# Feed-forward layers in two halves, with gate/up products of 512 columns over both parts of a normalised input

## The chip, the cores and the metric

The kernel runs on one NeuronCore of one Trainium2 chip. The time is the device time of one execution in microseconds (us), given as the median of several runs. The engines are TensorE (PE, with its weight loads shown apart as PEld), VectorE (DVE), ScalarE (ACT), GpSimd (POOL) and SyncE (SP, which issues most DMAs).

## What is computed

Two blocks of one model, 256 tokens (L) of width 1024 (D), in float32. Block one has four gated feed-forward layers around a Mamba-2 layer and a block-attention layer; block two has a conformer convolution, a sparse attention and, behind each, a feed-forward layer with a causal convolution of width 3. The part that matters here, cut from the reference:

```python
D_MODEL, SEQ, D_FF = 1024, 256, 2816

def modulate(x, g, c_act, w, b):
    m = c_act @ w + b                          # w: 1024 x 3072
    shift, scale, gate = jnp.split(m, 3, axis=-1)
    return rmsnorm(x, g) * (1.0 + scale[:, None, :]) + shift[:, None, :], gate[:, None, :]

def swiglu(h, w_gate, w_up, w_down):
    return (jax.nn.silu(h @ w_gate) * (h @ w_up)) @ w_down

# block one, for each of two depths: ffn, mixer (mamba2, then moba), ffn
h, g = modulate(x, norm_g[i, 0], c_act, mod_w[i, 0], mod_b[i, 0])
x = x + 0.5 * g * swiglu(h, ffn_w_gate[i, 0], ffn_w_up[i, 0], ffn_w_down[i, 0])

# block two, for each of two depths: mixer (conformer, then nsa), conv_ffn
def conv_ffn(h, w_up, w_dw, b_dw, w_down):
    a, v = jnp.split(h @ w_up, 2, axis=-1)
    return (jax.nn.silu(causal_dwconv(a, w_dw, b_dw)) * v) @ w_down
x = x + conv_ffn(rmsnorm_2(x, ffn_norm_g[i]), ffn_w_up[i], ffn_w_dw[i], ffn_b_dw[i], ffn_w_down[i])
```

## The kernel before

The residual X stays on the chip as eight tiles of 128 features by 256 tokens. Ten layers run one after the other: ffn0, ssm, ffn1, ffn2, moba, ffn3, conf, cffn0, nsa, cffn1; six of them are feed-forward layers (FFNs), the four gated ones of block one and the two with a convolution (cffn). All weights come as one stream of slots of 128x2048 float32 (1 MB), loaded by SP into a ring of six. An FFN takes 33 slots: 22 of gate/up (slot f holds the gate and the up columns of hidden tile f, of 22) and 11 of down.

**Precision by parts.** Each float32 operand is split into a high part of fewer bits and the rest. ACT writes w_hi of each slot (`high`, L1442), DVE writes w_lo (`low`, L1876), each into one of three buffers. A product is then three products that add up in PSUM: high by high, high weight by low input, low weight by high input. `woven` (L721) does this for gate and up together (six matmuls for each of eight k), `three` (L728, L729, L730) for down. All inputs have 256 columns, and in the gated FFNs 258: two further columns carry the shift of the modulation. "Triple" below means the three products of one weight tile.

**The input is not normalised ahead.** The gate/up products run on X times its gain (Hs_hi, Hs_lo); the sums of squares (L765) and the reciprocal root of each token (`rstd`, spread over the partitions by L709, written to `row` by ACT L1464) come while the first tiles are multiplied. ACT copies a finished tile from PSUM (L1456), POOL multiplies both halves by `row` (L651), ACT applies silu (L1473), DVE multiplies by the other half (L2086, or L2074 and following with the taps of the convolution), ACT rounds the result to hid_hi (L1477) and DVE writes hid_lo (L2095).

**Rounds.** After two gate/up slots and `clear` (L774: four matmuls of 512 bf16 columns that write zeros into the accumulators `acc`), a hardware loop runs rounds of two gate/up slots and one down slot; each down slot adds two hidden tiles into all eight output tiles in `acc`. All eight are finished in the last slot, and DVE then updates X.

**Folds.** The modulation vectors (c_act times a 1024x3072 matrix) are made on DVE beside this: a fold is two passes over 128x1024 (L1891) on a slot that POOL loads into a ring of its own (L568). In a round they stand after the slots 2, 4 and 7 of six (FOLD_AT).

The engines are ordered by hand, each by its own program text, and joined by semaphores: `split_ready` (weights split), `pair_free` (gate/up PSUM read), `hid_ready` (hidden parts written), `slot_done` (PE is done with a slot).

## Time and profile before

| quantity | value |
|---|---|
| median of 3 runs | 1868.75 us (1866.8 to 1869.99) |
| span of the profiled execution | 1865.1 us |
| PE busy | 1803.1 us, 97% of the span |
| DVE busy | 1323.5 us, 71% |
| ACT busy | 948.5 us, 51% |
| POOL busy | 377.5 us, 20% |
| DMA | 371.1 MB, mean 199 GB/s |

The profiled execution's span is 3.65 us under the median of the three runs. "Busy" of PE counts the time in which a matmul is in the array; records of neighbouring matmuls overlap, so the spacing of their starts says what one costs, and not the duration of a record. Idle time in brackets at a row's end is time in which the engine waited, with the instruction that released it.

### The profile page before, as it was taken

The page shows a single profiled execution, that of the slowest core. Times are in us where ns is not written, and L with a number is a line of the kernel's source. Part 1 is how long each engine was busy: PE and PEld are TensorE (multiplying, and loading weights), DVE is VectorE, ACT ScalarE, POOL GpSimd, SP SyncE. Part 2 cuts the span into 40 slices and gives each one's busy share as a digit, 9 for nine tenths or more (in the row PEclk, how much of TensorE's full clock was granted, in tenths as well). Part 3 has the DMA queues.
Part 4 walks back from the last instruction along what each step waited for, and adds up shares of the span by engine and source line. Part 5 has one row for each costly group of instructions (what it writes and reads, how often), then busy time and mean ns, then how long its engine had stood idle before and what let it go on. Part 6 is the DMA issues. An engine that isn't in the chain of part 4 may idle for free.

```text
span 1865.1 us, 36260 instructions
## 1 busy us (share of the span) xinstructions
PE 1803.1 (97%) x14574; PEld 1733.4 (93%) x14574; DVE 1323.5 (71%) x1824; ACT 948.5 (51%) x1357; POOL 377.5 (20%) x371
## 2 busy tenths in 40 slices
PE   3999999999999999999999999999999999999998
PEld 2999989979999999999889999988999989689998
DVE  6677877888767576768876555897666767866665
ACT  3554555474645465446465445316544533764453
POOL 1222200051222122211143221002222200431221
PEclk9999999999999999999999999999999999999999
DMA  9877835745577647675924554313555533134551
GB/s 376 319 274 279 324 113 181 277 151 226 184 290 264 256 179 293 253 279 177 372 92 161 188 191 180 142 62 114 177 183 180 180 143 133 41 109 167 191 187 67
DMA packets 51059, 371.10 MB, mean 199 GB/s; under 512 B 5664, under 2 KB 5664, under 8 KB 6048
## 3 DMA queue, kind: packets, MB, share of 16 engines
q1 hardware_dynamic: 41760, 302.85, 44.4%
q0 software_dynamic: 9216, 67.11, 9.2%
q8 instruction: 56, 0.92, 0.2%
q14 instruction: 27, 0.22, 0.0%
HBM read 368.89 MB, written 1.05 MB: 198 GB/s over the span
## 4 chain that ended last, share of the span: by engine, by line
PE 83%; DVE 10%; ACT 4%; issue 1%; DMA 1%; POOL 0%; POOLq 0%; SPq 0%; DVEq 0%; ACTq 0%
PE gu L721 39%; PE acc L729 8%; PE acc L728 8%; PE acc L730 8%; DVE arena L2424 3%; PE gu L1054 2%; PE gu L1193 2%; PE gu L728 2%; PE gu L730 2%; PE gu L729 2%; DVE w_lo L1876 2%; DMA mring<-in_mods 1%; DVE mring L1891 1%; DVE arena L2166 1%; PE acc L1264 1%
## 5 line engine op out<-in xcount | busy, mean ns | idle before, releaser
L1876 DVE TENSOR_TENSOR w_lo<-ring,w_hi 128x2048 fp32r<-128x2048 f32 x265 | 613.7, 2319 | 271.6 <-ACT w_hi L1442 271.5
L1442 ACT ACTIVATE w_hi<-ring 128x2048 fp32r<-128x2048 f32 x265 | 504.9, 1907 | 74.6 <-PE acc L730 49.3
L721 PE MATMUL gu<-Hs_hi,w_hi 128*128 128x258 f32 (+1 forms) x2112 | 427.8, 284 | 2.5 <-DVE Hs_lo L1940 1.3
L721 PE MATMUL gu<-Hs_lo,w_hi 128*128 128x258 f32 (+1 forms) x2112 | 423.1, 282 | 0.0
L721 PE MATMUL gu<-Hs_hi,w_lo 128*128 128x258 f32 (+1 forms) x2112 | 422.5, 281 | 0.0
L651 POOL TENSOR_TENSOR arena<-arena,rstd 128x512 f32<-128x512 f32 x132 | 201.0, 1523 | 831.1 <-ACT arena L1456 778.4
L721 PEld LDWEIGHTS gu<-Hs_hi,w_hi 128*128 128x128 f32 x2112 | 325.7, 189 | 4.8 <-issue 1.8
L721 PEld LDWEIGHTS gu<-Hs_hi,w_lo 128*128 128x128 f32 x2112 | 325.8, 189 | 0.0
L721 PEld LDWEIGHTS gu<-Hs_lo,w_hi 128*128 128x128 f32 x2112 | 325.4, 189 | 0.0
L729 PE MATMUL acc<-hid_lo,w_hi 128*128 128x256 f32 x1056 | 297.8, 282 | 0.0
L728 PE MATMUL acc<-hid_hi,w_hi 128*128 128x256 f32 x1056 | 296.4, 281 | 1.2 <-DVE hid_lo L2095 1.2
L730 PE MATMUL acc<-hid_hi,w_lo 128*128 128x256 f32 x1056 | 295.8, 280 | 0.0
L1477 ACT ACTIVATE hid_hi<-arena 128x256 fp32r<-128x256 f32 x132 | 55.2, 419 | 292.2 <-DVE arena L2086 201.6
L728 PEld LDWEIGHTS acc<-hid_hi,w_hi 128*128 128x128 f32 x1056 | 198.9, 188 | 1.5 <-issue 1.5
L730 PEld LDWEIGHTS acc<-hid_hi,w_lo 128*128 128x128 f32 x1056 | 199.4, 189 | 0.0
L729 PEld LDWEIGHTS acc<-hid_lo,w_hi 128*128 128x128 f32 x1056 | 198.4, 188 | 0.0
L1891 DVE SCALAR_TENSOR_TENSOR mring<-mring,cact 128x1024 f32<-128x1024 f32 x144 | 170.0, 1220 | 11.1 <-DMA mring<-in_mods 10.9
L1456 ACT ACTIVATE arena<-gu 128x516 f32<-128x516 f32 (+1 forms) x132 | 78.4, 594 | 138.2 <-PE gu L721 135.0
L728 PE MATMUL gu<-H_hi_ssm,w_hi 128*128 128x256 f32 x384 | 109.8, 286 | 4.9 <-DVE w_lo L1876 3.1
L2095 DVE TENSOR_TENSOR hid_lo<-arena,hid_hi 128x256 fp32r<-128x256 f32 x132 | 70.0, 530 | 57.6 <-ACT hid_hi L1477 57.6
L730 PE MATMUL gu<-H_hi_ssm,w_lo 128*128 128x256 f32 x384 | 108.4, 282 | 0.0
L729 PE MATMUL gu<-H_lo,w_hi 128*128 128x256 f32 x384 | 108.2, 282 | 0.0
(413 smaller groups left out, 2841.5 us busy)
## 6 DMA issues: line engine op xcount, KB each, us to landing
ring<-in_weights SPq DMA_DIRECT2D x276, 1024.0 KB, 4.8
mring<-in_mods POOLq DMA_DIRECT2D x64, 1024.0 KB, 6.1
mring<-in_mods SPq DMA_DIRECT2D x8, 1024.0 KB, 7.5
con<-in_constants SPq DMA_DIRECT2D x1, 1408.0 KB, 12.1
X<-in_x SPq DMA_DIRECT2D x1, 1024.0 KB, 7.2
out<-X SPq DMA_DIRECT2D x1, 1024.0 KB, 3.9
cact<-in_c SPq DMA_DIRECT2D x1, 512.0 KB, 3.3
vec<-in_vectors SPq DMA_DIRECT2D x1, 498.0 KB, 4.1
```

The lines of the kernel that those rows point to most:

```text
L651: pool.tensor_tensor(both, both, row.unsqueeze(1).to_broadcast([P, 2, L]), ALU.mult).then_inc(scaled_ready, 1)
L721: ins = mm(dst, part, x_lo if i == 1 else x_hi, start=start and i == 0, stop=stop and i == 2, skip_group_check=True)
L728: mm(dst, hi, x_hi, start=start, stop=False, skip_group_check=True)
L729: mm(dst, hi, x_lo, start=False, stop=False, skip_group_check=True)
L730: return mm(dst, lo, x_hi, start=False, stop=stop, skip_group_check=True)
L1442: act.activation(w_hi[buffer_of(n0, s)][:, :], ring[:, n % RING, :], ACT.Copy).then_inc(hi_ready, 1)
L1456: act.activation(c[:, :, 0:width], gu[:, 2 * (f % 2):2 * (f % 2) + 2, 0:width], ACT.Copy).then_inc(pair_free, 1)
L1477: act.activation(hid_hi[:, f % 4, :], a, ACT.Copy).then_inc(hid_hi_ready, 1)
L1876: dve.tensor_tensor(w_lo[b][:, :], ring[:, n % RING, :], w_hi[b][:, :].bitcast(F32), ALU.subtract).then_inc(split_ready, 1)
L1891: ins = dve.scalar_tensor_tensor(out=w, in0=w, scalar=1.0, in1=cact[:, :], op0=ALU.mult, op1=ALU.mult, accum_out=total)
L2095: dve.tensor_tensor(hid_lo[:, f % 4, :], o, hid_hi[:, f % 4, :].bitcast(F32), ALU.subtract).then_inc(hid_ready, 1)
L2424: ins = dve.scalar_tensor_tensor(out=part_sum, in0=UP[:, m, tap:tap + L], scalar=v1("w_dw", tap * KD + m), in1=part_sum, op0=ALU.mult, op1 ...
```

## The change

In all six FFNs the order of the slots, the form of the products and the place of the normalisation change.

- **Two halves.** Gate/up tiles 0 to 11, then six slots of down over them, gate/up 12 to 21, then five slots of down. Down runs output tile by output tile (`down_tiles`), each into one of four banks of `acc` (its columns 0 to 255), still by three products of 256 columns; `start=True` opens a bank, `clear` is gone. Each output tile is added to X twice (`partial`), once for each half. The hardware loops of the FFNs are unrolled.
- **512 columns.** Tiles 0 to 2 run as before, on the bare input, the third into two banks of `acc`. Meanwhile Hs_hi and Hs_lo are overwritten, k by k, by the parts of the normalised input (DVE `scaled` L2300, ACT `normal` L1646, DVE `normal_low` L2311). From tile 3 on (19 of 22), `paired` multiplies w_hi by both parts in one product of 512 columns (L837; an access pattern with a step from Hs_hi to Hs_lo) and w_lo by the high part in one of 256 (L839). The two halves of a PSUM bank are added later: ACT copies one to SBUF (`low_half` L1596), DVE adds the other (`add` L2284).
- **Other engines.** The multiplication of gate and up (L728 of the new kernel) and the low hidden part (L734) move from DVE to POOL; POOL's scaling by `row` (L718) remains for the three bare tiles. In the cffn layers the first tap moves from DVE to ACT.
- **Folds** stand at the slots of FOLD_SLOTS: in ffn0 16 of them, eight of these in the adjacent slots 19 to 26; in ffn1 and ffn2 12 each, with 19 to 22 and 24, 25 adjacent.
- **Ends of layers.** The squares and entries of the next layer and the splitting of its first two slots are placed in the last down slots. The diagonals of one of the three homes of the conformer's taps are built behind ffn3. Some buffers move, and the weight stream is packed in the new order.

```diff
-FOLD_AT = (2, 4, 7)
-LAST_FOLDS = (2, 3, 4, 5)
+FOLD_SLOTS = {"ffn0": (3, 5, 7, 9, 11, 13, 15, 17, 19, 20, 21, 22, 23, 24, 25, 26),
+              "ffn1": (5, 7, 9, 11, 14, 16, 19, 20, 21, 22, 24, 25),
+              "ffn2": (5, 7, 9, 11, 14, 16, 19, 20, 21, 22, 24, 25)}
+HALF_F0, HALF_N = (0, 12), (12, 10)
+DOWN_SLOT, DOWN_N = (12, 28), (6, 5)
...
+            def paired(bank, w, cols, x_both, x_hi, start, stop):
+                mm(bank.rearrange("p (a t) -> p a t", a=2), w_hi[w][:, cols], x_both, start=start, stop=False,
+                   skip_group_check=True)
+                return mm(bank[:, 0:L], w_lo[w][:, cols], x_hi, start=False, stop=stop, skip_group_check=True)
...
-                    pe.wait_ge(split_ready, s0 + s + 1 + it * 6)
-                    if f >= 2:
-                        pe.wait_ge(pair_free, f0 + f - 1 + it * 4)
+                    pe.wait_ge(split_ready, s0 + s + 1)
+                    pe.wait_ge(pair_free, f0 + (f - 2 if f < BARE_F + 2 else f - 1))
+                    for k in range(KD):
+                        if f == BARE_F:
+                            state["nh"] += 1
+                            pe.wait_ge(nh_ready, state["nh"])
+                        for e, cols in enumerate(columns(k)):
+                            ins = paired(bank[:, e, :], buffer_of(n0, s), cols, hs_twin(k), Hs_hi[:, k, 0:L],
+                                         start=(k == 0), stop=(k == KD - 1))
...
-                gate_up(1)
-                clear()
-                with pe.Fori(0, ROUNDS) as it:
-                    for s in (2, 5):
-                        gate_up(s, it)
-                        gate_up(s + 1, it)
-                        down(s + 2, (s - 2) // 3, it)
-                down(FSLOTS - 1, PAIRS - 1, last=True)
+                bare_gate_up(1)
+                bare_gate_up(2)
+                for f in range(BARE_F, HALF_F0[1]):
+                    gate_up(f)
+                down(0)
+                for f in range(HALF_F0[1], NF):
+                    gate_up(f)
+                down(1)
...
+                def low_half(f):
+                    act.wait_ge(slot_done, n0 + gu_slot(f) + 1)
+                    act.wait_ge(mul_ready, hid0 + f - 1)
+                    act.activation(cp[:, f % 2, :, 0:L], bank_of(f)[:, :, L:2 * L], ACT.Copy).then_inc(half_taken, 1)
...
+                def add(f):
+                    dve.wait_ge(half_taken, (NF - BARE_F) * i + f - BARE_F + 1)
+                    c = cp[:, f % 2, :, 0:L]
+                    dve.tensor_tensor(c, bank_of(f)[:, :, 0:L], c, ALU.add).then_inc(pair_free, 1)
...
+                for s in range(BARE_F, DOWN_SLOT[1]):        # DVE
+                    f = GU_TILE.get(s)
+                    if f is not None:
+                        add(f)
+                        low(n0, s + 2)
...
+                    fold_at(s)
```

PE at the start of ffn0 before, from the spread of the root on (names: w_hi_56 and w_lo_59 are one of the three pairs of buffers):

```order
L709 MATMUL acc<-con,rtok 128x128
L721 MATMUL gu<-Hs_hi,w_hi_55 128x258 x2
L721 MATMUL gu<-Hs_lo,w_hi_55 128x258 x2
L721 MATMUL gu<-Hs_hi,w_lo_58 128x258 x2
...
L774 MATMUL acc<-zeros 128x512 x3
L774 MATMUL acc<-zeros 128x512 [waits row_ready]
...
L721 MATMUL gu<-Hs_hi,w_hi_56 128x258 [waits pair_free]
L721 MATMUL gu<-Hs_hi,w_hi_56 128x258
L721 MATMUL gu<-Hs_lo,w_hi_56 128x258 x2
L721 MATMUL gu<-Hs_hi,w_lo_59 128x258 x2
```

And in the changed kernel, the end of the third tile and the start of the fourth (HL holds Hs_hi and Hs_lo):

```order
L824 MATMUL acc<-HL,w_hi_53 128x258 x4
L824 MATMUL acc<-HL,w_lo_56 128x258 x2
L837 MATMUL gu<-HL,w_hi_51 128x512 [waits nh_ready,pair_free,split_ready]
L839 MATMUL gu<-HL,w_lo_54 128x256
L837 MATMUL gu<-HL,w_hi_51 128x512
L839 MATMUL gu<-HL,w_lo_54 128x256
L837 MATMUL gu<-HL,w_hi_51 128x512 [waits nh_ready]
L839 MATMUL gu<-HL,w_lo_54 128x256
```

Six products of 258 columns for a k have become four, two of 512 and two of 256; the clears are gone, and the fourth tile waits for the normalised input k by k.

DVE at the same place before, from the reciprocal root to the second hidden tile:

```order
L2059 RECIPROCAL rtok<-rtok 128x2
L1876 TENSOR_TENSOR w_lo_57<-ring,w_hi_54 128x2048
L2086 SCALAR_TENSOR_TENSOR arena<-arena 128x256
L2095 TENSOR_TENSOR hid_lo<-arena,hid_hi 128x256
L1876 TENSOR_TENSOR w_lo_58<-ring,w_hi_55 128x2048
L2086 SCALAR_TENSOR_TENSOR arena<-arena 128x256
L2095 TENSOR_TENSOR hid_lo<-arena,hid_hi 128x256
```

DVE there in the changed kernel, where five further pairs of L2300 and L2311 are left out:

```order
L2334 RECIPROCAL rtok<-rtok 128x2
L2117 TENSOR_TENSOR w_lo_54<-ring,w_hi_51 128x2048
L2300 SCALAR_TENSOR_TENSOR arena<-X,modsc,rstd 128x256 x2
L2311 SCALAR_TENSOR_TENSOR HL<-arena,modv,HL 128x256
...
L2300 SCALAR_TENSOR_TENSOR arena<-X,modsc,rstd 128x256
L2311 SCALAR_TENSOR_TENSOR HL<-arena,modv,HL 128x256 x2
L2117 TENSOR_TENSOR w_lo_55<-ring,w_hi_52 128x2048
L2284 TENSOR_TENSOR arena<-gu,arena 128x2x256
L2117 TENSOR_TENSOR w_lo_56<-ring,w_hi_53 128x2048
L2132 SCALAR_TENSOR_TENSOR mring,modraw<-mring,cact 128x1024 x2
```

Sixteen steps of the normalisation now stand between the third and the fourth w_lo, and each further w_lo stands behind the addition of a tile two slots earlier.

POOL in ffn0 before, a scaling for each tile and a load of the next matrix slot for each fold:

```order
L651 TENSOR_TENSOR arena<-arena,rstd 128x2x256
L568 DMA mring<-in_mods 128x2048
L651 TENSOR_TENSOR arena<-arena,rstd 128x2x256
L568 DMA mring<-in_mods 128x2048
L651 TENSOR_TENSOR arena<-arena,rstd 128x2x256 x2
```

POOL in the changed kernel, from the row of the root to the first load behind a fold:

```order
L718 TENSOR_TENSOR arena<-arena,rstd 128x2x256 x2
L725 TENSOR_TENSOR arena<-arena 128x256
L728 TENSOR_TENSOR arena<-arena 128x256
L725 TENSOR_TENSOR arena<-arena 128x256
L728 TENSOR_TENSOR arena<-arena 128x256
L718 TENSOR_TENSOR arena<-arena,rstd 128x2x256
L734 TENSOR_TENSOR HL<-arena,HL 128x256 x2
L725 TENSOR_TENSOR arena<-arena 128x256
L728 TENSOR_TENSOR arena<-arena 128x256
L734 TENSOR_TENSOR HL<-arena,HL 128x256
L728 TENSOR_TENSOR arena<-arena 128x256
L734 TENSOR_TENSOR HL<-arena,HL 128x256
```

L725 adds the shift of the bare tiles. POOL now takes part twice in every hidden tile, in one chain with ACT.

## Rows read from the trace of the kernel before

**Rows 1.** The page, busy time by engine.

```profile
PE 1803.1 (97%) x14574; PEld 1733.4 (93%) x14574; DVE 1323.5 (71%) x1824; ACT 948.5 (51%) x1357; POOL 377.5 (20%) x371
```

**Rows 2.** Timeline of PE, two gate/up slots and a down slot (start, duration, instruction).

```profile
103.24 0.41 PE L721 MATMUL gu<-Hs_hi,w_hi 128*128 128x258 f32 x2
...
114.68 0.28 PE L728 MATMUL acc<-hid_hi,w_hi 128*128 128x256 f32 x1
```

**Rows 3.** Windows: length; busy PE, PEld, DVE, ACT, POOL; PEclk, DMA share, GB/s.

```profile
103.24:120.33 17.09, 17.09 (x146) 17.09 (x145) 11.06 (x12) 8.54 (x10) 3.84 (x4) 1.00 0.82 317
1325.37:1342.43 17.06, 17.06 (x147) 17.06 (x145) 11.04 (x14) 8.45 (x11) 4.25 (x3) 1.00 0.54 185
```

**Rows 4.** Timeline of PE, the clears of ffn0.

```profile
51.08 1.04 PE L774 MATMUL acc<-zeros 128*128 128x512 bf16 x4
51.78 0.59 PE L721 MATMUL gu<-Hs_hi,w_hi 128*128 128x258 f32 x2
```

**Rows 5.** Line L1107, plain float32 matmuls: duration ns min/median/max, first and last start.

```profile
L1107 PE MATMUL gu<-arena,ring x96: 379/379/379, 1196.1 to 1216.6; 128*128 128x256 f32 x96
```

**Rows 6.** Groups by line and shape: count, busy us, mean ns, idle before.

```profile
L1876 DVE TENSOR_TENSOR w_lo<-ring,w_hi 128x2048 fp32r<-128x2048 f32 x265 | 613.7, 2319 | 271.6 <-ACT w_hi L1442 271.5
L1891 DVE SCALAR_TENSOR_TENSOR mring<-mring,cact 128x1024 f32<-128x1024 f32 x144 | 170.0, 1220 | 11.1 <-DMA mring<-in_mods 10.9
L2521 DVE TENSOR_TENSOR arena<-gu,arena 128x512 f32<-128x512 f32 x8 | 5.5, 689 | 4.7 <-PE gu L1193 3.5 <-ACT arena L1768 1.2
L1442 ACT ACTIVATE w_hi<-ring 128x2048 fp32r<-128x2048 f32 x265 | 504.9, 1907 | 74.6 <-PE acc L730 49.3 <-DMA ring<-in_weights 23.2 <-PE acc L1165 1.3
L1456 ACT ACTIVATE arena<-gu 128x516 f32<-128x516 f32 x88 | 52.7, 599 | 131.3 <-PE gu L721 128.2
L1477 ACT ACTIVATE hid_hi<-arena 128x256 fp32r<-128x256 f32 x132 | 55.2, 419 | 292.2 <-DVE arena L2086 201.6 <-DVE arena L2084 90.6
L605 POOL TENSOR_TENSOR arena<-arena,H 128x256 f32<-128x256 f32 x12 | 9.1, 761 | 6.4 <-DVE H L2209 6.4
```

**Rows 7.** Line L651, POOL's scaling: duration ns min/median/max, first and last start.

```profile
L651 POOL TENSOR_TENSOR arena<-arena,rstd x132: 1186/1198/2826, 49.6 to 1849.4; 128x512 f32<-128x512 f32 x132
```

**Rows 8.** Timeline of POOL and DVE where the two meet.

```profile
1708.22 2.83 POOL L651 TENSOR_TENSOR arena<-arena,rstd 128x512 f32<-128x512 f32 x1 [7.23 <-ACT arena L1456]
...
1707.69 2.29 DVE L1876 TENSOR_TENSOR w_lo<-ring,w_hi 128x2048 fp32r<-128x2048 f32 x1 [1.38 <-ACT w_hi L1442]
...
1020.21 1.27 POOL L627 TENSOR_TENSOR mring<-con,vec 128x640 f32<-128x640 f32 x1
...
1020.82 2.81 DVE L1876 TENSOR_TENSOR w_lo<-ring,w_hi 128x2048 fp32r<-128x2048 f32 x1 [1.87 <-ACT w_hi L1442]
```

**Rows 9.** Timeline of PE and ACT at the start of ffn1.

```profile
471.24 0.41 PE L721 MATMUL gu<-Hs_hi,w_hi 128*128 128x258 f32 x2
...
476.96 1.39 PE L765 MATMUL acc<-ones,arena 128*128 128x1 f32 x12
482.26 0.49 PE L721 MATMUL gu<-Hs_hi,w_hi 128*128 128x258 f32 x2
...
482.54 0.38 ACT L1464 ACTIVATE rstd<-acc 128x256 f32<-128x256 f32 x1 [2.08 <-PE acc L709]
```

**Rows 10.** Timeline of PE: idle time between layers, and in the mixers.

```profile
229.92 3.71 PE L699 MATMUL gu<-ones,H 128*128 128x1 f32 x20 [1.21 <-DVE H L1900]
...
1479.84 0.35 PE L728 MATMUL acc<-hid_hi,w_hi 128*128 128x256 f32 x1 [0.77 <-DVE hid_lo L2095]
...
272.88 0.39 PE L728 MATMUL gu<-H_hi_ssm,w_hi 128*128 128x256 f32 x1 [2.08 <-DVE w_lo L1876]
...
421.85 0.69 PE L897 MATMUL gu<-arena 128*64 128x256 f32 x2 [2.36 <-DVE H L2209]
```

**Rows 11.** Windows behind the last two of these; PEclk is the granted clock.

```profile
421.90:425.30 3.40, 3.40 (x17) 2.82 (x18) 3.33 (x8) 1.63 (x4) 1.65 (x2) 0.50 0.00 0
...
272.90:276.30 3.40, 3.40 (x29) 3.40 (x30) 3.09 (x12) 2.24 (x2) 0.00 (x0) 1.00 0.62 263
```

744 lines of the change are left out of this document (467 added, 277 removed).

## The prediction, made before the changed kernel ran

> **What bounds the kernel now.** I read the page's busy times first, then PE's timeline in the feed-forward layers, then what happens at their starts. PE is busy 97% of the span [rows 1], and a round of two gate/up slots and one down slot is filled with matmuls without a gap, in both kinds of FFN [rows 3]. So within an FFN the time is the number of products times their spacing, and every other engine has slack: DVE 11.06 of 17.09 us, ACT 8.54, POOL 3.84 [rows 3]. The spacing: 96 products of 258 columns lie between 103.24 and 114.68 [rows 2], 0.1192 us each, a triple 0.3575. The rest of the round, 17.09 - 11.44 = 5.65 us for 48 products of 256 columns, is 0.1177 each [rows 2, 3]. With this in the cffn round, its gate/up triple is (17.06 - 5.65)/32 = 0.3566. What the change can win is PE time; what it can lose is PE waiting where it now never waits.
>
> **The price of a 512-column product.** It is not in the trace in this form. Nearest is the clear, 512 columns of bf16: four begin at 51.08, and the pair of products behind them is recorded from 51.78 with 0.59 us in place of 0.41, so it really begins about 0.18 later: 0.88/4 = 0.22 [rows 2, 4]. Plain float32 products of 256 columns, 96 from 1196.1 to 1216.6, stand 20.5/95 = 0.216 apart [rows 5]; that these are 256 columns passed twice is my reading, since they take nearly twice the 0.1177. Lower bound 0.216, upper bound twice a 256-column product, 0.2354. I take 0.2185, between the two rows, which both move as many columns or passes and lie far from the upper end. A triple becomes 0.2185 + 0.118 = 0.3365; by the upper end, 0.3534.
>
> The trace's own spacing says that a short product pays some 0.01 us beyond its columns, which the wide one pays once. The Trainium skill, "TensorE: Matmul & The Clock Gate", section "Back-to-back issue gap", gives an isolated product as N/2.4 ns plus 2.5. That is 109 ns for 256 columns and 216 for 512, so a pair would save 2.5 ns of a triple. The rows disagree for 256 columns (117.7) and agree for 512; by that rule for both, the gain below would be 1824 x 0.0025 = 4.6 us in place of 37.7.
>
> **Part 1, the wide products.** 19 tiles x 16 = 304 triples for each FFN. Gated: 304 x (0.3575 - 0.3365) = 6.4, four times 25.5. cffn: 304 x (0.3566 - 0.3365) = 6.1, twice 12.2. Together **-37.7**, all on PE's path.
>
> **Part 2, clears and ends.** Four clears of 0.22 in six FFNs go: **-5.3** [rows 4]. The last down slot of cffn0 waits 0.77 for hidden parts, which under the new order are needed later, and squares of the next layer made inside the last down slots take away the 1.21 before 229.92 [rows 10]: **-2.0**. Down itself keeps its products, 0.1177 each. The second update of X, eight of about 0.5 us on DVE for each FFN, lies in down slots of 5.65, where DVE otherwise has one w_lo of 2.3 and at most a fold: nothing. Unrolling: nothing. Gross **-45.0**.
>
> **Part 3, the joins.** This is where waits are added. Let T be the first product of a gated FFN. A bare tile is 48 x 0.119 = 5.72; the second one ends at T + 13.1 (482.26 is T + 11.0, with three of its eight steps to go) [rows 2, 9], the third at T + 18.8. Wide tiles then take 16 x 0.3365 = 5.4, so the fifth (tile 4) is due at T + 24.2 and tile 5 at T + 29.6. `row` is now asked for two steps earlier: T + 10.1 [rows 9]. The chain that decides goes through all engines, each step by [rows 6, 7], with what is queued ahead: ACT copies tile 1, 13.7; three `normal`, 15.9; the w_hi queued there, 17.7; five more `normal` alternating with DVE's `scaled` and `normal_low`, 0.8 for each, 21.3; silu of tile 1, 21.8; POOL's shift and multiplication, 0.73 each, 23.2; ACT's copy of tile 2, 24.1; POOL's scaling 1.2, 25.3; its low part 26.0, which silu of tile 2 awaits, 26.5; two on POOL, 28.0; hid_hi 28.5; `low_half` of tile 3, 29.0; DVE's `add`, like L2521 0.7, 29.7; w_lo of tile 5, 31.9. PE waits **2.3** for that. Behind the waiting w_lo nothing else is late for PE: slack returns in tile 6.
>
> That is the sum without contention. With it: L651 takes 1.19 alone and up to 2.83, and in [rows 8] it ends 1.07 after the L1876 that had begun before it; the other way round, an L1876 that meets a running POOL step takes 2.81 in place of 2.29. The two run one after the other. "SBUF — State Buffer" in the Trainium skill, section "SBUF: two separate sides", says the same: one port pair, held for a whole instruction, where DVE reads two inputs from SBUF against a POOL step that reads SBUF; the trace agrees. The chain above has six POOL steps, and DVE's w_lo, `scaled` and folds are between them. POOL's shift holds off the w_lo of tile 4, which comes at T + 26.4, 2.2 late, and w_lo of tile 5 comes 3.0 after that tile's new due time: **5.2** in all. In the cffn layers silu waits for taps on ACT and DVE, and the same working gives 2.1 and 5.3. I take 4.5 for each of six, near the upper end since [rows 8] is plain: **+27** (13 to 31).
>
> **Part 4, folds.** In a slot with a fold DVE needs 0.6 for `add`, 2.2 for w_lo and 2 x 1.14 for the fold, 5.1 of 5.4; before, no more than one slot in two had a fold. POOL has 2 x 0.73, not at once with the latter two. Where folds are adjacent that is 5.9 to 6.5 against PE's 5.4, after some slack is used: up to 8 in ffn0 (eight in a row), 2 each in ffn1 and ffn2; nothing if POOL's steps fall into DVE's waits. Of 0 to 12 I take **+6**. The loads do not bind: a weight and a matrix slot for each 5.4 us is 390 GB/s, about 317/0.82 = 387, what the DMA gives at full share [rows 3], and the rings are six and three slots ahead.
>
> **Part 5, the clock.** Behind a wait of 2.36 us PE ran at granted clock 0.50 (1.2 GHz) for 3.4 us, behind one of 2.08 at 1.00 (2.4 GHz) [rows 10, 11]. A spell costs 3.4/2 = 1.7. New waits are of 2 to 3 us, and there may be twelve: 0 to 7, taken **+4**, as the two rows are one of each kind and most waits are of the shorter.
>
> Sum: 1865.1 - 45.0 + 27 + 6 + 4 = 1857.1 for the span, plus the 3.65 by which the median stands above it: **1860.8 us**.
>
> **Rivals.** *A: POOL and DVE hardly meet.* Then the joins cost 13, folds nothing, the clock 0 to 2: 1865.1 - 45.0 + 14 + 3.65 = 1838. For it: most of the 132 scalings take 1.19, the median [rows 7]. Against it: they are timed by PE and now POOL's steps double and lie in a chain. *B: they meet everywhere, and the cold clock follows.* Joins 31, folds 12, clock 7: net +5, 1873.8, slower. For it: rows 8. It decides once all waits together pass 48.7 us (45.0 and the 3.7 that can be told), which the folds must supply. *C: a 512-column product costs twice one of 256.* Place: all 1824 triples; the gain of 37.7 falls to 304 x (4 x 0.0041 + 2 x 0.0032) = 6.9, so +30.8; wide tiles last 0.27 longer, which takes some 6 from the waits: 1885.6, up to 1892. My -7.9 is used up at a triple of 0.341, and the kernel is slower by over 3.7 from 0.343. For it: nothing in these rows but the missing form; against it rows 4 and 5. The Trainium skill's formula would end near the same time, 1893.9; the rows for 256 columns speak against it. *D: the change does not do what it says,* for instance the access pattern over two tensors is read slower than a plain one, or the splitting of the next layer's slots is late at the ends: slower by some us, no more seen in this trace.
>
> **How the numbers follow.** What a measurement of this kernel can tell from no change is about 0.2%, 3.7 us: faster is under 1865.0, slower over 1872.5. The forecast case (waits of 28 to 46, 1852 to 1870) has 0.42: 0.29 faster, 0.13 same. A has 0.20, all faster. B 0.18: 0.05 same, 0.13 slower. C 0.13, slower. D 0.07: 0.02 same, 0.05 slower. Faster 0.49, same 0.20, slower 0.31. The range takes in most of A down to 1836 and of C up to 1886.
>
> **What would show it.** PE's timeline: a wide and a narrow product every 0.3365 us (C: 0.353). The waits before L837 at tiles 4 and 5 of each FFN, 2 to 3 us each, released by DVE's w_lo; one at tile 5 only under A. L2117 with many records near 2.8 to 3.5, and POOL's L728 and L734 near 1.5 to 2.9 (A: 2.29 and 0.73). Waits at slots 20 to 26 of ffn0. Half-clock windows behind waits. I am wrong if PE waits at another place: at the nh_ready waits of tile 3, where the normalisation is only just in time, or where down opens a bank that DVE has not yet added to X.

## The result, and the profile after

| | before | after |
|---|---|---|
| median | 1867.78 us (4 runs, 1865.88 to 1869.99) | 1878.40 us (4 runs, 1876.26 to 1881.19) |
| ratio | 1 | 1.0063, 95% interval 1.0049 to 1.0077 |
| span of the profiled execution | 1865.1 | 1874.5 |
| PE busy | 1803.1 (97%) | 1796.3 (96%) |
| DVE, ACT, POOL busy | 1323.5, 948.5, 377.5 | 1374.7, 973.0, 509.0 |

The change made the kernel slower by 10.6 us, 0.6%, and the interval lies clear of 1; 1860.8 had been forecast, and faster. The page's busy line of after stands against [rows 1]: PE is busy 7 us less where some 40 had been forecast, and the span is 9.4 longer. So PE's work hardly shrank, and PE waits 16 us more.

```profile
PE 1796.3 (96%) x12724; PEld 1643.4 (88%) x12726; DVE 1374.7 (73%) x1774; ACT 973.0 (52%) x1449; POOL 509.0 (27%) x533
```

**The wide products.** PE's timeline of after in a stretch without waits (start, duration, instruction), and below it line L837 in the window of three tiles of ffn1, with the starts of its first and last record:

```profile
499.01 0.39 PE L837 MATMUL gu<-HL,w_hi 128*128 128x512 f32 x1
499.24 0.28 PE L839 MATMUL gu<-HL,w_lo 128*128 128x256 f32 x1
499.36 0.40 PE L837 MATMUL gu<-HL,w_hi 128*128 128x512 f32 x1
...
L837 PE MATMUL gu<-HL,w_hi x49: 387/397/403, 513.9 to 530.9; 128*128 128x512 f32 x49
```

From 499.01 to 499.36 is one triple, and 48 of them lie between 513.9 and 530.9: 0.354 us each, of which the wide product has 0.235 and the narrow one 0.119. [rows 2, 3] had 0.3575. The forecast wanted 0.3365. This is rival C of the prediction, its price to the nanosecond.

**The waits.** The same timeline at tile 5 of ffn1, at tile 4 of ffn0 and in a cffn layer; then ACT, POOL and DVE in the 12 us ahead of tile 5 of ffn1. The bracket is idle time and what ended it.

```profile
505.70 0.50 PE L837 MATMUL gu<-HL,w_hi 128*128 128x512 f32 x1 [3.01 <-DVE w_lo L2117]
...
62.17 0.50 PE L837 MATMUL gu<-HL,w_hi 128*128 128x512 f32 x1 [0.16 <-DVE w_lo L2117]
...
1343.35 0.50 PE L837 MATMUL gu<-HL,w_hi 128*128 128x512 f32 x1 [1.02 <-DVE w_lo L2117]
...
493.94 0.49 ACT L1624 ACTIVATE arena<-arena 128x256 f32<-128x256 f32 x1
...
494.47 2.28 DVE L2117 TENSOR_TENSOR w_lo<-ring,w_hi 128x2048 fp32r<-128x2048 f32 x1
...
494.51 2.72 POOL L725 TENSOR_TENSOR arena<-arena 128x256 f32<-128x256 f32 x1 [5.77 <-ACT arena L1624]
497.30 0.64 POOL L728 TENSOR_TENSOR arena<-arena 128x256 f32<-128x256 f32 x1
...
502.14 0.58 ACT L1596 ACTIVATE arena<-gu 128x512 f32<-128x512 f32 x1
...
502.76 0.69 DVE L2284 TENSOR_TENSOR arena<-gu,arena 128x512 f32<-128x512 f32 x1 [6.00 <-ACT arena L1596]
503.37 2.28 DVE L2117 TENSOR_TENSOR w_lo<-ring,w_hi 128x2048 fp32r<-128x2048 f32 x1
```

The reader sees the forecast chain: silu of tile 1 at 493.94, POOL's shift, its multiplication, and so on to ACT's `low_half` at 502.14, DVE's `add` at 502.76 and w_lo at 503.37, which PE gets at 505.70. POOL's shift takes 2.72 where its like takes 0.6, because DVE began a w_lo 0.04 us earlier. Read in this way, 2.0 of the 3.0 us are the meeting of the two engines and 1.0 is the length of the chain; `dvebare` below tests it. The wait is there in all four gated layers (3.0, 3.0, 3.0, 3.8); tile 4, for which 2.2 had been forecast, waits 0.16 to 0.78; each cffn layer waits 1.0 twice and 0.4 in the second half of down. The gated layers have no wait in down, and none at slots 20 to 26.

**The clock.** Windows behind the waits of 3 us in ffn0, ffn1 and ffn2 (length; busy time of PE, PEld, DVE, ACT, POOL; PEclk; DMA):

```profile
71.10:74.50 3.40, 3.40 (x11) 2.92 (x12) 3.40 (x5) 2.23 (x2) 1.57 (x2) 0.52 0.38 161
505.70:509.00 3.30, 3.30 (x19) 2.88 (x20) 2.75 (x2) 2.53 (x3) 2.77 (x2) 1.00 0.38 161
698.10:702.50 4.40, 4.40 (x16) 3.71 (x17) 2.73 (x2) 2.53 (x3) 3.38 (x3) 0.61 0.29 117
```

PEclk is a mean: 0.52 is nearly all of the window at 1.2 GHz (0.50), 1.00 is 2.4 GHz, and 0.61 is a spell of 3.4 us at 1.2 GHz within the 4.4. After waits of 3.0 us the granted clock is at its lower level in ffn0 and ffn2 and not in ffn1, and in ffn3 it is behind 3.8; tile 5 takes 7.22, 7.28 and 7.01 us there, 5.75 in ffn1. That is 4.5 us in three spells.

**The account of the spans**, from the lengths of all tiles and slots in the two traces (what a tile takes above its normal length holds the wait, the refill of some 0.2 behind each, and the clock):

| term | forecast | measured |
|---|---|---|
| wide products | -37.7 | -6.3 |
| clears | -5.3 | -5.3 (taken from the forecast) |
| starts and ends of layers | -2.0 | -5.5 |
| waits and refills, and 1.4 of waits of before gone | +33 | +20.8 |
| half clock behind them | +4 | +4.5 |
| down slots of ffn2 take 5.76 in place of 5.65 | 0 | +1.1 |
| sum | -8 | +9.3, and 9.4 in the spans |

The row of the starts and ends holds three things. 2.4 us are at the start of nsa, where waits of 0.48, 0.43 and 0.32 are gone. 1.9 are at the start of ssm. Before, the granted clock was at its lower level for 10.2 us there, most of the sums of squares among them (20 products in 3.71 us); after, it was so for 6.8 us that begin behind the sums (2.39 us). The last 0.9 stand ahead of the first product of ffn0, at 34.86 before and 33.94 after; all the other kernels begin it between 33.7 and 34.9, so this part is chance rather than the change.

### The profile page after: what moved, and what is told of

Same layout as the page of the kernel before. It is cut to its first block, busy times and chain, and to the rows that moved or that the text cites. A ratio compares the mean times of both kernels' runs of the same rounds, so it can differ in the third digit from the quotient of the medians.

```text
span 1874.5 us, 31471 instructions
## 1 busy us (share of the span) xinstructions
PE 1796.3 (96%) x12724; PEld 1643.4 (88%) x12726; DVE 1374.7 (73%) x1774; ACT 973.0 (52%) x1449; POOL 509.0 (27%) x533
## 4 chain that ended last, share of the span: by engine, by line
PE 79%; DVE 12%; ACT 4%; POOL 2%; issue 2%; DMA 1%; SPq 0%; POOLq 0%; ACTq 0%; DVEq 0%
PE acc L824 20%; PE gu L837 20%; PE gu L839 10%; PE gu L824 3%; DVE arena L2706 3%; PE gu L1320 3%; DVE w_lo L2117 3%; PE gu L1181 2%; PE gu L831 2%; PE gu L833 2%; PE gu L832 2%; PE acc L831 2%; PE acc L832 2%; PE acc L833 2%; DMA mring<-in_mods 1%
## 5 line engine op out<-in xcount | busy, mean ns | idle before, releaser
L837 PE MATMUL gu<-HL,w_hi 128*128 128x512 f32 x1824 | 651.2, 399 | 18.2 <-DVE w_lo L2117 18.2
L839 PE MATMUL gu<-HL,w_lo 128*128 128x256 f32 x1824 | 514.5, 282 | 0.0
L837 PEld LDWEIGHTS gu<-HL,w_hi 128*128 128x128 f32 x1824 | 344.9, 189 | 105.3 <-DVE w_lo L2117 22.0
L824 PE MATMUL acc<-HL,w_hi 128*128 128x256 f32 (+1 forms) x2304 | 405.8, 282 | 0.8 <-POOL HL L734 0.8
L824 PEld LDWEIGHTS acc<-HL,w_hi 128*128 128x128 f32 x2304 | 349.7, 189 | 1.7 <-POOL HL L734 1.2
L839 PEld LDWEIGHTS gu<-HL,w_lo 128*128 128x128 f32 x1824 | 346.7, 190 | 0.0
L824 PE MATMUL acc<-HL,w_lo 128*128 128x256 f32 (+1 forms) x1152 | 315.4, 281 | 0.0
L2284 DVE TENSOR_TENSOR arena<-gu,arena 128x512 f32<-128x512 f32 x114 | 78.5, 689 | 192.9 <-ACT arena L1596 192.9
L728 POOL TENSOR_TENSOR arena<-arena 128x256 f32<-128x256 f32 x132 | 137.4, 1041 | 291.6 <-ACT arena L1619 167.0
L824 PEld LDWEIGHTS acc<-HL,w_lo 128*128 128x128 f32 x1152 | 214.8, 189 | 0.0
L1596 ACT ACTIVATE arena<-gu 128x512 f32<-128x512 f32 x114 | 68.1, 598 | 260.5 <-PE gu L839 260.5
L2132 DVE SCALAR_TENSOR_TENSOR mring<-mring,cact 128x1024 f32<-128x1024 f32 x144 | 186.6, 1333 | 10.2 <-DMA mring<-in_mods 10.0
L734 POOL TENSOR_TENSOR HL<-arena,HL 128x256 fp32r<-128x256 f32 x132 | 115.6, 878 | 215.0 <-ACT HL L1631 215.0
```

The lines of the kernel that those rows point to most:

```text
L728: pool.tensor_tensor(o, o, b, ALU.mult).then_inc(mul_ready, 1)
L734: pool.tensor_tensor(hid_low(name, t), act_buf[:, f % 2, :], hid_hi[:, t, :].bitcast(F32), ALU.subtract).then_inc(hid_ready, 1)
L824: ins = mm(dst, part, x_lo if i == 1 else x_hi, start=start and i == 0, stop=stop and i == 2, skip_group_check=True)
L837: mm(bank.rearrange("p (a t) -> p a t", a=2), w_hi[w][:, cols], x_both, start=start, stop=False, skip_group_check=True)
L839: return mm(bank[:, 0:L], w_lo[w][:, cols], x_hi, start=False, stop=stop, skip_group_check=True)
L2132: ins = dve.scalar_tensor_tensor(out=w, in0=w, scalar=1.0, in1=cact[:, :], op0=ALU.mult, op1=ALU.mult, accum_out=total)
```

## The experiments

Each kernel was timed beside the kernel before on one chip; the ratio is to that. The kernel after had 1.0063, and "so much faster than after" compares the two ratios or medians. Each ratio has an interval of 0.1 to 0.2% to either side, so that differences under some 4 us between two changed kernels are not clear of noise.

### What a wide product costs

`rates` leaves out the computation. It runs 96 products of each form, with changing weights and nothing else at work, then DVE and POOL alone and together:

```diff
+            for i in range(N):  # R512
+                ins = pe.matmul(o(i, 512), w(Wr, i), R[:, 256:768], start=True, stop=True, skip_group_check=True)
...
+            for i in range(N):  # TWIN
+                ins = pe.matmul(ps[:, i % 4, :].rearrange("p (a t) -> p a t", a=2), w(Wr, i), R[:, 0:2048].rearrange("p (a t) -> p a t", a=2)[:, :, 0:256], start=True, stop=True, skip_group_check=True)
```

> This kernel leaves out the whole computation and only returns its input; it times runs of 96 products with changing weights, and then VectorE and GpSimd alone and together. Theory (width): a product of the rounded float32 type costs 0.461 ns for each column at any width, so 118 ns for 256 columns, 177 for 384, 236 for 512, whether the 512 columns lie together or in two ranges. Rival (two ranges): 512 columns that lie together cost about 218 ns and only the pattern with a step from one part to the other costs 236. Under both, bf16 products of 512 columns cost about 218 and plain float32 products of 256 about 216. For the other engines: a VectorE subtraction of 128x2048 takes 2.29 us alone and a GpSimd product of 128x256 some 0.63 to 0.73 alone; if one excludes the other, VectorE records of 2.8 or more and GpSimd records of 2 or more appear when both run, and none with a PSUM input on VectorE.

Its lines, with duration in ns and the starts of first and last: rounded float32 of 256, 512 and 384 columns, bf16 of 512, plain float32 of 256 (two records for a product).

```profile
L75 PE MATMUL ps<-R,Wr x96: 283/283/284, 31.9 to 43.3; 128*128 128x256 f32 x96
L77 PE MATMUL ps<-R,Wr x96: 389/389/398, 43.4 to 65.0; 128*128 128x512 f32 x96
L79 PE MATMUL ps<-R,Wr x96: 333/334/346, 65.2 to 81.7; 128*128 128x384 f32 x96
L95 PE MATMUL ps<-Rb,Wb x94: 379/379/380, 185.9 to 206.2; 128*128 128x512 bf16 x94
L97 PE MATMUL ps<-big,Wf x192: 379/379/380, 206.4 to 247.6; 128*128 128x256 f32 x192
```

Spacings from start to start: 120.0, 226.7 and 173.3 ns for 256, 512 and 384 columns; 226.7 for the two-range pattern as well; 112 for 128 and 192 columns; 216 for bf16 of 512 and 109 of 256; 215.8 for a record of plain float32. Neither theory stands as written. The pattern is innocent. The rounded type does not cost a fixed 0.461 ns a column either: 120, 173.3 and 226.7 lie on one line, 0.4167 ns a column and 13.3 ns for each product. bf16 of 512 columns pays 2 to 3 ns beside 0.4167 for each of its columns. With weights of 32 columns a rounded product of 256 takes 113.3 and one of 512 takes 231.6, so the 13 ns are no constant of the type. The bf16 and plain float32 rows on which the forecast stood ([rows 4, 5]) were rows of another form, without the 13 ns; and a wide product should have won 13 ns a triple in a pure stream, 360 to 347. Plain float32 of 256 columns is two records of 215.8 for each product, 431.6 against 109.3 of bf16: four times as much, and not twice, as I had read [rows 5] and expected here.

`mixes` leaves out the computation as well and asks why the kernel has 354 and not 347:

> This kernel leaves out the whole computation and only returns its input; it times mixtures of products of 512 columns (W) and 256 columns (N), rounded float32, all with changing weights. Alone they took 226.7 and 120 ns, and alternating 355 for a W and an N, 8 more than their sum. Theory (alternation costs): every pattern in which W and N take turns costs 354 to 356 for a pair, whatever the bank, and grouped patterns (four and four, sixteen and sixteen) fall to 347. Rival (a bank written twice in a row costs): the cost goes with the bank and not with the order; then grouped patterns stay at 355 and W alone in one bank for 16 in a row is dearer than 226.7.

```profile
L81 PE MATMUL ps<-R,Wr x64: 395/398/403, 65.0 to 87.2; 128*128 128x512 f32 x64
...
L90 PE MATMUL ps<-R,Wr x64: 392/394/400, 110.3 to 132.2; 128*128 128x512 f32 x64
```

A wide and a narrow product in turn take 353.4 (63 spacings from 65.0 to 87.2), 236.3 and 117.0; narrow first and else the same 346.7 (231.8 and 114.9); two and two 348.7; four and four 350.6; sixteen and sixteen 348.0. The bank makes no difference. In the like stream of `rates` the spacings repeat with a period of three pairs: 233, 117, 241, 120, 236, 113. Both theories miss. Wide first and narrow first are the same sequence but for its start, and differ by 6.7 ns: the cost hangs on something finer than the order, which these runs don't name. It stays open, and so does whether narrow first would save anything in the kernel, where it was not tried.

`grouped` takes the order into the kernel:

```diff
                         for e, cols in enumerate(columns(k)):
-                            ins = paired(bank[:, e, :], buffer_of(n0, s), cols, hs_twin(k), Hs_hi[:, k, 0:L],
-                                         start=(k == 0), stop=(k == KD - 1))
+                            wide(bank[:, e, :], buffer_of(n0, s), cols, hs_twin(k), start=(k == 0))
+                    for k in range(KD):
+                        for e, cols in enumerate(columns(k)):
+                            ins = narrow(bank[:, e, :], buffer_of(n0, s), cols, Hs_hi[:, k, 0:L], stop=(k == KD - 1))
```

> The changed kernel with the same products in another order: in each gate/up tile first the sixteen of 512 columns, then the sixteen of 256. Theory (alternation costs 8 ns for each pair): a tile falls from 5.66 to 5.55 us, 114 tiles, some 12 us of TensorE time, of which the waits before tiles 4 and 5 take back 0.2 to 0.4 in each layer: 1867 to 1869. Rival (order is nothing): 1878.

1875.72 us, ratio 1.0043 (1.0027 to 1.0059). A tile falls from 5.66 to 5.63, a wide product behind a wide one takes 232.5 on the mean, not 226.7. The theory had the sign and a quarter of the size; 114 tiles by 0.03 is 3 us. The medians differ by 2.7, which agrees, but by itself would not be clear of noise.

`narrow` takes the wide product away and leaves all else:

```diff
-                mm(bank.rearrange("p (a t) -> p a t", a=2), w_hi[w][:, cols], x_both, start=start, stop=False,
-                   skip_group_check=True)
+                mm(bank[:, 0:L], w_hi[w][:, cols], x_hi, start=start, stop=False, skip_group_check=True)
+                mm(bank[:, L:2 * L], w_hi[w][:, cols], x_lo, start=False, stop=False, skip_group_check=True)
```

> The changed kernel with each 512-column product cut into two of 256 columns, into the same two halves of the bank; all else as it is. Theory (width costs in proportion): a triple stays at 0.354 us, the time is that of the changed kernel, 1878, within 2 us. Rival (the wide product still brings something of the 0.017 us each that was forecast): 1824 x 0.01 = 18 us slower, 1890 or more.

1883.47 us, ratio 1.0093 (1.0076 to 1.0110): some 5.6 us slower than after, between the two expectations. That is 3.0 ns for each of 1824 triples, and the trace agrees: a tile takes 5.71 in place of 5.66. This is what the wide product is worth in this kernel, a seventh of the forecast.

### What TensorE waits for

`rates` again, DVE's subtraction of 128x2048 and POOL's product of 128x256: alone (the group's busy time and mean ns), then DVE with POOL beside it, then DVE with a PSUM input and POOL beside it.

```profile
L112 DVE TENSOR_TENSOR lo<-X,big 128x2048 f32<-128x2048 f32 x8 | 17.7, 2283 | 330.7 <-remote 330.7
L138 POOL TENSOR_TENSOR pc<-pa,pb 128x256 f32<-128x256 f32 x8 | 5.5, 722 | 15.4 <-DVE lo L112 15.4
...
L112 DVE TENSOR_TENSOR lo<-X,big 128x2048 f32<-128x2048 f32 x12 | 32.3, 2763 | 5.4 <-POOL pc L138 5.4
L138 POOL TENSOR_TENSOR pc<-pa,pb 128x256 f32<-128x256 f32 x13 | 33.6, 2613 | 0.1
...
L122 DVE TENSOR_TENSOR lo<-pd,sc 128x512 f32<-128x512 f32 x12 | 7.3, 683 | 3.3 <-POOL pc L138 3.3
L138 POOL TENSOR_TENSOR pc<-pa,pb 128x256 f32<-128x256 f32 x17 | 11.7, 728 | 0.1
```

The means of the second pair take in steps that met nothing. Where both run they take strict turns: DVE's records go from 2.28 to 2.81 (0.53 more, against 0.68 from one POOL step to the next alone), POOL's from 0.72 to 2.77, nearly as long as DVE's. With DVE's input in PSUM, POOL keeps its 0.73 and DVE has 0.68. This is as expected. The rule cited in the prediction, from "SBUF — State Buffer" in the Trainium skill, section "SBUF: two separate sides", holds here: by these records a step of two SBUF inputs on DVE and a POOL step exclude each other for a whole instruction. Six steps of one SBUF input on DVE (TENSOR_SCALAR, 128x2048) with POOL beside them took 9.54 us, the first 1.23 and the others 1.74 each: they are held up too.

`direct` puts all three products into one half of the bank; ACT copies the sum and the addition on DVE is gone:

```diff
-                mm(bank[:, L:2 * L], w_hi[w][:, cols], x_lo, start=False, stop=False, skip_group_check=True)
+                mm(bank[:, 0:L], w_hi[w][:, cols], x_lo, start=False, stop=False, skip_group_check=True)
...
-                        add(f)
                         low(n0, s + 2)
```

> The changed kernel with all three products of a weight tile in one half of the bank, 256 columns each, so that ScalarE copies the finished sum and VectorE adds nothing. Theory (a chain through ScalarE, GpSimd and VectorE sets the wait before tile 5, and the wide product brings nothing): PE's time is unchanged, the waits of 3.0 us before tile 5 fall by the 0.7 of the addition in each feed-forward layer, and with them some spells at half clock: 1869 to 1875. Rival (the waits come from contention alone and stay): 1878.

```profile
506.56 0.36 PE L837 MATMUL gu<-HL,w_hi 128*128 128x256 f32 x1 [2.01 <-ACT arena L1596]
...
72.08 0.36 PE L837 MATMUL gu<-HL,w_hi 128*128 128x256 f32 x1 [3.99 <-ACT arena L1596]
...
59.79 4.90 DVE L2117 TENSOR_TENSOR w_lo<-ring,w_hi 128x2048 fp32r<-128x2048 f32 x2
```

1875.61 us, ratio 1.0052 (1.0035 to 1.0069), a little above the theory's span of times, since the wide products' 5.6 us are lost here too; against `narrow`, its proper neighbour, it is 7.9 us faster. The wait in ffn1, ffn2 and ffn3 is 2.0, and its releaser is now ACT's copy itself: without the addition the w_lo is ready in time, and the same chain is late at its last but one member. In ffn0 the wait rose to 4.0: with nothing between them, two w_lo and a fold follow each other on DVE, and POOL's shift, its multiplication, its scaling and two low parts take 2.7, 2.6, 2.2 and 2.4 us, where after had 2.7, 0.6, 1.2 and 1.4. The clock fell behind this wait and behind none of the three of 2.0.

`dvebare` gives the multiplications of the three bare tiles in the gated layers back to DVE, shift included:

```diff
-                    if f < BARE_F and name[0] != "c":
-                        pool.tensor_tensor(b, b, cp[:, f % 2, 1, L:L + 1].to_broadcast([P, L]),
-                                           ALU.add).then_inc(bias_ready, 1)
...
+                def mul_bare(f):
+                    dve.wait_ge(silu_ready, SILU_AT[name] + f + 1)
+                    o, b = act_buf[:, f % 2, :], cp[:, f % 2, 1, 0:L]
+                    dve.scalar_tensor_tensor(out=o, in0=b, scalar=cp[:, f % 2, 1, L:L + 1], in1=o,
+                                             op0=ALU.add, op1=ALU.mult).then_inc(mul_ready, 1)
...
+                if not conv:
+                    mul_bare(0)
+                    mul_bare(1)
                 low(n0, 4)
...
+                else:
+                    mul_bare(2)
```

> The changed kernel with the multiplications of the three bare tiles of the four gated layers back on VectorE, in one step each with the shift; GpSimd keeps the rest. In the changed kernel's trace GpSimd's shift of tile 1 stood 2.0 us behind a VectorE step that began 0.04 us earlier, in the chain to the w_lo for which TensorE waits 3.0 us at tile 5. Theory (exclusion 2.0, length of the chain 1.0): the wait falls to 0 to 1.2 in the four layers, and the half-clock spells behind it go: 9 to 12 us faster than the changed kernel, 1866 to 1869. Rival (another member of the chain, ScalarE's copy or the additions, is nearly as late): the wait falls by less than 1, 1875 to 1878.

```profile
503.74 0.50 PE L835 MATMUL gu<-HL,w_hi 128*128 128x512 f32 x1 [0.82 <-DVE w_lo L2115]
```

1868.35 us, ratio 1.0000 (0.9991 to 1.0010): 10.0 us faster than after, as the theory said. At tile 5, 0.8 is left of the 3.0 us in three layers, and 1.6 in ffn3, and no spell at half clock stands behind it. Some of the wait moved to tile 4, which has 0.6 where it had 0.2 (1.2 for 0.8 in ffn3): from the first product of ffn1 to tile 5 it is 32.1 us in place of 33.9. So six POOL steps in each gated layer, with their meeting with DVE and the clock behind it, are worth as much as the whole loss of 10.6. Without them the change is even with the kernel before; it still wins nothing, because the wide products bring so little.

`warm` leaves the wait and fills it:

```diff
+                    if f == 5 and name[0] != "c":
+                        for _ in range(12):
+                            mm(acc[:, 2, :], zeros[:, 0:P], zeros[:, 0:1].to_broadcast([P, 512]), start=True, stop=True,
+                               skip_group_check=True)
                     pe.wait_ge(split_ready, s0 + s + 1)
```

> The changed kernel with twelve clearing products of 512 bf16 columns into an unused bank ahead of tile 5 of the four gated layers; at full clock they fill 2.6 us of the 3.0 in which TensorE waits. Theory (three of the four waits are followed by half clock, at 1.3 to 1.6 us each): those spells go, the wait itself stays, 3.5 to 5 us faster than the changed kernel: 1873.5 to 1875. Rival (the clock falls for another reason than this wait): 1878 or a little over.

Its timeline at tile 5 of ffn1 and its windows behind that point in ffn0 and ffn2:

```profile
501.93 2.78 PE L872 MATMUL acc<-zeros 128*128 128x512 bf16 x12
505.10 0.50 PE L837 MATMUL gu<-HL,w_hi 128*128 128x512 f32 x1 [0.38 <-DVE w_lo L2121]
...
71.30:74.70 3.40, 3.25 (x18) 2.84 (x19) 3.40 (x6) 2.23 (x2) 1.74 (x2) 1.00 0.45 188
697.30:701.70 4.40, 4.23 (x23) 3.67 (x24) 2.91 (x3) 2.53 (x3) 3.58 (x3) 1.00 0.35 149
```

1872.81 us, ratio 1.0038 (1.0028 to 1.0049), some 5 us faster than after, the upper end of the theory's 3.5 to 5. The last wait is the same, 2.78 filled and 0.38 left, and the clock stays at its upper level in these windows, and in that of ffn3: the half-clock spells are the price of the waits on top of the waits.

`swap` changes the order of two steps in DVE's loop:

```diff
-                        add(f)
                         low(n0, s + 2)
+                        add(f)
```

> The changed kernel with one pair of steps in the other order: in each gate/up slot VectorE splits the weights of the slot two ahead first and adds the two halves of the finished tile after that. Theory (the w_lo of tile 5 is ready to be made 6 us before it is, and only stands in VectorE's queue behind the addition of tile 3, which the long chain holds up): the wait before tile 5 of the gated layers falls from 3.0 to about 0.8 us, which the addition itself then sets, and no spell at half clock follows; 10 to 13 us faster than the changed kernel, 1865 to 1868. Rival (contention of VectorE with GpSimd sets the wait whatever the order): 1875 or more.

PE at tile 5 of ffn1, POOL and DVE ahead of it:

```profile
504.70 0.47 PE L837 MATMUL gu<-HL,w_hi 128*128 128x512 f32 x1 [2.86 <-DVE arena L2284]
...
493.66 2.72 POOL L725 TENSOR_TENSOR arena<-arena 128x256 f32<-128x256 f32 x1 [5.77 <-ACT arena L1624]
496.46 2.56 POOL L728 TENSOR_TENSOR arena<-arena 128x256 f32<-128x256 f32 x1
...
493.62 4.90 DVE L2117 TENSOR_TENSOR w_lo<-ring,w_hi 128x2048 fp32r<-128x2048 f32 x2
...
503.86 0.69 DVE L2284 TENSOR_TENSOR arena<-gu,arena 128x512 f32<-128x512 f32 x1 [5.34 <-ACT arena L1596]
```

1874.5 us, ratio 1.0051 (1.0037 to 1.0064): within noise the time of after, and 0.5 from the rival's 1875. The theory missed. The rival had contention set the wait whatever the order; it does here, but through a new meeting that the new order brings. The w_lo is early now, just as meant, but it stands directly behind another, and POOL's shift and its multiplication are both held up, 2.72 and 2.56. The chain comes 1.9 us later, and PE waits 2.86 for the addition. The first w_lo cost the chain 2 us; moving the second forward cost it 2 more.

### Parts of the change, and other ways to it

`noclear` is the kernel before with one part, the clears gone:

```diff
+                        if first and m == 6:
+                            pe.wait_ge(row_ready, i + 1)
...
-                                        hid_hi[:, h, :], hid_lo[:, h, :], start=False, stop=False)
+                                        hid_hi[:, h, :], hid_lo[:, h, :],
+                                        start=first and e == 0 and m % 2 == 0, stop=False)
...
-                clear()
-                with pe.Fori(0, ROUNDS) as it:
+                for s in (2, 5):
+                    gate_up(s)
+                    gate_up(s + 1)
+                    down(s + 2, (s - 2) // 3, first=s == 2)
+                with pe.Fori(1, ROUNDS) as it:
```

> The kernel before with one part of the change: the four clearing products of each feed-forward layer are gone, and the first product into each bank starts it instead (the first round stands outside the hardware loop for this). Theory: PE is the bound there and nothing else is late, so the 6 x 4 products of 0.22 us come off in full: 5.3 us faster than before, 1862.5. Rival: the last bank holds the row of the root until ScalarE has read it, or another wait takes the place: 0 to 2 us faster.

```profile
1327.71 0.39 PE L721 MATMUL gu<-Hs_hi,w_hi 128*128 128x256 f32 x1 [0.48 <-DVE w_lo L1882]
```

1862.95 us, ratio 0.9980 (0.9970 to 0.9990), 3.4 us faster than before, between theory and rival. The gated layers shorten by 0.7 to 2.1 each (the 2.1 of ffn0 also hold a spell at half clock at 43.0 that before has and this run has not); the first cffn layer gives nearly all back in a new wait of 0.48 for w_lo. The account above takes the full 5.3 for this term, which is by so much uncertain.

`halves` keeps the halves and drops the wide products and the normalisation in place:

```diff
+                for f in range(NF):
...
+                    scale(f)
                     while done < len(folds) and gu_slot(f) > folds[done]:
...
                         load_mods(n, n + 1)
...
+                        ins = woven([bank_of(f)[:, e, 0:width] for e in range(2)], buffer_of(n0, s), columns(k),
+                                    Hs_hi[:, k, 0:width], Hs_lo[:, k, 0:width], start=(k == 0), stop=(k == KD - 1))
...
+                    low(n0, s + 3)
                     if f is not None:
...
+                        mul(f)
+                        fold_at(s)
+                        low_hidden(f)
```

> The changed kernel without its wide products: all 22 tiles run on the bare input in three products of 258 columns, nothing is normalised in place, scaling is on GpSimd and multiplication and low part on VectorE as before the change; the two halves, the order of down, the missing clears and the work placed in the last down slots stay, and the folds are spread over gate/up and down slots. Theory (the wide products bring 3 ns a triple, 5.5 us in all, and cost the waits; the rest of the change, clears and ends, brings 9 to 10): no waits in the layers, 1857 to 1861. Rival (folds or scaling now make VectorE late somewhere in the gated layers): 1864 or more, with waits released by w_lo.

```profile
161.99 0.58 PE L801 MATMUL gu<-HL,w_hi 128*128 128x258 f32 x1 [12.62 <-DVE w_lo L2030]
```

1921.92 us, ratio 1.0295 (1.0281 to 1.0309): the rival came, by far more than it said, and the theory's time was not reached. I had put folds into the down slots, while POOL loads the next matrix slots only behind its scaling of tile 12, which comes after down: DVE stands in a fold whose data isn't asked for, and PE waits 12.6 us. Further waits of 1.0 to 3.6 us stand in down in all layers. The run says nothing on its question, what the halves bring alone; that stays open.

`late` has four bare tiles and orders the start of a layer by what is needed first; `late_swap` is `late` with the exchange of `swap` and one more of the kind on ACT:

```diff
-        BARE_F = 3
+        BARE_F = 4
...
+                for m in range(3):
                     normal_low(m)
...
+                    scaled(m + 3)
+                if not conv:
+                    mul_bare(2)
...
+                for m in range(3, KD):
+                    normal_low(m)
...
+                low(n0, 5)
+                if not conv:
+                    mul_bare(3)
```

and `late_swap` against `late`:

```diff
-                        add(f)
                         low(n0, s + 2)
+                        add(f)
...
-                    silu(3)
                     high(n0, 6)
+                    silu(3)
```

> The changed kernel with one more bare tile (four, then 18 of 22 tiles by 512 columns), the bare tiles multiplied on VectorE in the gated layers, and the steps at the start of each layer put in the order in which the tiles need them: hidden tiles 0 to 2 go through before or within the normalisation, and only tile 3 stands behind it. Theory (what is lost are the waits at tiles 4 and 5, because the normalisation of all eight k is queued in front of the hidden tiles): nearly all of the 12 us of waits that are left with the bare tiles on VectorE go, for 0.05 us a layer of dearer products: 1856 to 1860. Rival (the engines are simply full in this stretch and the wait moves to another tile): 1864 or more.

> The kernel late (four bare tiles, bare tiles multiplied on VectorE) with the same exchange of split and addition, and ScalarE's w_hi of slot 6 ahead of the silu of tile 3. Theory: late's wait of 1.2 us before tile 6 had the same cause, a w_lo behind an addition, and goes; about 0.4 us is left in each layer: 1858 to 1863, faster than both kernels. Rival (VectorE is full there): the wait comes back at tile 7 or 8, 1868 or more.

`late`, then `late_swap`, PE at the places with the longest waits of ffn1:

```profile
507.28 0.50 PE L838 MATMUL gu<-HL,w_hi 128*128 128x512 f32 x1 [1.19 <-DVE w_lo L2129]
```

```profile
499.25 0.50 PE L838 MATMUL gu<-HL,w_hi 128*128 128x512 f32 x1 [0.37 <-DVE w_lo L2129]
```

`late` took 1870.6 us, ratio 1.0022 (1.0013 to 1.0031): the rival was right, the wait had moved to tile 6, again a w_lo behind an addition that the chain held up. `late_swap` took 1857.47 us, ratio 0.9957 (0.9943 to 0.9970), 8 us faster than before and some 12 faster than `late`. Here the exchange works: the w_lo stands where DVE had idled 2.1 us for the addition, a multiplication stands between it and the w_lo ahead of it, and the POOL step that it holds up (2.28 us for a low part) is behind the chain. Each gated layer waits 0.4 us in all, the cffn layers 0.4 and 1.0. That this arrangement is the reason is read from the two traces; no run separates it from the exchange on ACT.

## Why the prediction was wrong, by its own steps

**The price of a 512-column product** is the step that failed. It took 0.2185, "between the two rows, which both move as many columns or passes"; the wide product takes 0.235. The rows were of other forms: bf16 pays 2 to 3 ns beside its columns, a plain float32 product takes two records, while the rounded type pays 13 ns for a product in a pure stream and 22 here (0.235 less 512 columns at 0.4167 ns, 0.213). The text itself named the upper end, 0.3534 for a triple, and gave it 0.13 as rival C, with "nothing in these rows but the missing form" for it. That form should have had more weight: no row of the trace showed a rounded product of more than 256 columns in a stream. The only wider ones, of 384 columns, stand singly in the ssm layer:

```profile
386.17 0.42 PE L919 MATMUL acc<-cum_r,sel_r 128*128 128x384 f32 x1
386.43 0.28 PE L922 MATMUL acc<-mask_bf,id_bf 128*128 128x256 bf16 x1
386.47 0.42 PE L919 MATMUL acc<-cum_r,sel_r 128*128 128x384 f32 x1
```

From the first to the third it is 0.30 us (0.32 at another such place). 384 columns at 0.4167 ns are 0.160, and the bf16 product takes 0.109: 0.27 together. That was a hint at the dearer price, though not a clean row.

Part 1 was -37.7 and came out at -6.3, which alone turns -8 into +23. That the span grew by 9.4 only is luck: the terms of waits and folds were 12 too large and the gain at the ends 3.5 too small, and with 1.6 on the other side they hid 14 of the 31 us.

**Part 2** was right in sign for the clears, 3 to 5, and named the wrong places for the ends. The wait of 1.21 ahead of ssm is still 0.98, and the 0.77 in cffn0 is 0.39 at another place; the 5.5 came mostly from the start of nsa, from the clock at the start of ssm, and in part from chance.

**Part 3**, the joins, had the mechanism: the chain, its members, the exclusion and the wait of 3.0 at tile 5 are as forecast. Its make-up is not: the chain alone was given 2.3, and 1.0 is its share by the reading above, with 2.0 for one meeting; that the sum came out at 3.0 is in part luck. The wait of 2.2 at tile 4 did not come. DVE's w_lo began 0.04 us ahead of POOL's shift and not after it, and was done 24.9 us after T, where 26.4 had been forecast; but in the other order it would have been later by the 0.5 of a meeting, not by 1.5, so that figure was too late in either order. Wide tiles that last 5.66 leave more time as well. With the cffn layers 20 to 22 were measured, of 27.

**Part 4**, folds, cost nothing of 6. They were sized against a slot of 5.4 us that became 5.66. One of the adjacent fold slots of ffn0:

```profile
168.80:174.46 5.66, 5.66 (x34) 4.92 (x33) 5.66 (x7) 3.01 (x4) 2.54 (x3) 1.00 0.94 353
```

DVE is busy for 5.66 of 5.66 us here and in the slots around it: it just keeps pace, without any slack. By this row DVE could not have followed slots of 5.4, so that at the forecast price of the wide products the cost of Part 4 would have been due. The two terms were not independent; no run shows that case.

**Part 5** was right: 4.5 for 4, three spells behind waits of 3 us and more.

**The rivals.** C gave 1885.6 with waits of 31; it came with 25, and the time was 1878.4. The case was the right one with its costs too high; its chance of 0.13, and the 0.31 for slower as a whole, were too low for a price of which no row showed the form.

## What to carry to other kernels

A change that trades three instructions for two stands or falls with the price of the new one; take it from a row of the same type and weight form, or time a hundred of them alone before anything is built on it. Where two engines exclude each other, look not only at how often they meet but at which chain the loser stands in: 2 us of one POOL step became 3 us of TensorE, and then a spell at half clock. The order of two steps in a queue can be worth more than their cost: with one exchange on DVE and one on ACT, `late_swap` is 12 us faster than `late`, while the exchange on DVE does nothing in `swap`. And an engine that is full only just fits: a faster TensorE can make it the one that everybody waits for.
